# Sample latents turned by VectorE, with the first sequence's chain earlier, and a merge with a filled edge and shorter column sums

## The reference

```
def one_seq(args):
    q_b, pt, c_b, kr_b = args
    c_all = concatenate([cache_latent[layer, pt].reshape(past_len, KV_LORA), c_b])
    kr_all = concatenate([cache_krope[layer, pt].reshape(past_len, QK_ROPE), kr_b])
    k = mla_keys(c_all, kr_all, kpos, w_uk, g_k_mla)      # rms_norm over each head's 96 columns
    return attend_latent(q_b, k, c_all, qpos, kpos, w_uv) # softmax, context in latents, then w_uv
```

```
y = silu(layer_norm(conv(hist) + b_dw, g_ln, b_ln)) @ w_conv_out
x = x + (sig(g_a) * y_mla + sig(g_b) * y_conv + sig(g_c) * y_mem) @ w_out
```

## Time and profile before

| what | value |
|---|---|
| median of 3 runs | 2519.83 us |
| the profiled execution's own time | 2512.91 us |
| its span, first to last instruction | 2511.1 us |
| TensorE busy | 2418.1 us (96%) |
| VectorE, ScalarE, GpSimd busy | 1044.8, 597.2, 768.6 us |
| mean granted TensorE clock | 0.990 |

### The profile page before, as it was taken

One profiled execution on the slowest core, in us unless ns is written; L12 is line 12 of the kernel. 1 busy time (PEld: TensorE's weight loads), 2 busy tenths in 40 slices (PEclk: granted clock), 3 DMA queues, 4 the chain that ended last, 5 costly groups with the idle time before them and its releaser, 6 DMA issues. The chain is left out here.

```text
span 2511.1 us, 35803 instructions
## 1 busy us (share of the span) xinstructions
PE 2418.1 (96%) x12532; PEld 1641.9 (65%) x12532; DVE 1044.8 (42%) x2299; ACT 597.2 (24%) x1193; POOL 768.6 (31%) x574
## 2 busy tenths in 40 slices
PE   7999999999899999999999999989999999999996
PEld 4566666666654555556656666647778777877874
DVE  4233344445524343349964226643333332333331
ACT  2222333334333444210012101201111111112121
POOL 1000000000025555300000005544556555656652
PEclk9999999999999999999999999999999999999998
DMA  8111111011233232063112162048999999999996
GB/s 290 40 41 45 45 45 42 28 31 38 68 113 89 75 90 65 20 192 77 41 51 77 38 208 68 19 178 297 331 332 332 344 352 358 357 363 358 365 353 188
DMA packets 208870, 404.65 MB, mean 161 GB/s; under 512 B 51675, under 2 KB 139024, under 8 KB 192220
## 3 DMA queue, kind: packets, MB, share of 16 engines
q1 hardware_dynamic: 173220, 318.41, 36.1%
q0 software_dynamic: 27936, 72.22, 11.5%
q10 hardware_dynamic: 7536, 11.73, 1.3%
HBM read 342.83 MB, written 70.70 MB: 165 GB/s over the span
## 5 line engine op out<-in xcount | busy, mean ns | idle before, releaser
L2488 POOL DMA_INDIRECT mergedT<-tokens_normed,gather_rows x304 | 309.3, 1018 | 120.5 <-issue 94.8
L2687 PEld LDWEIGHTS pGe<-xT,we_g 128*128 128x128 f32 x2048 | 261.8, 191 | 33.2 <-issue 32.8
L2602 DVE STREAM_TRANSPOSE xT<-mergedT 128x1280 f32<-128x1280 f32 (+2 forms) x64 | 152.7, 2386 | 283.9 <-DMA mergedT<-tokens_normed,gather_rows 263.0
L2687 PE MATMUL pGe<-xT,we_g 128*128 128x128 f32 (+4 forms) x2048 | 270.8, 290 | 0.0
L2687 PE MATMUL pUe<-xT,we_u 128*128 128x128 f32 (+4 forms) x2048 | 267.0, 289 | 0.0
L2687 PEld LDWEIGHTS pUe<-xT,we_u 128*128 128x128 f32 x2048 | 260.7, 191 | 0.0
L1437 PE MATMUL pKs<-ws_uk,cTs 128*128 128x512 f32 x512 | 233.2, 597 | 1.2 <-issue 1.2
L1150 POOL TENSOR_TENSOR rk<-ssk,half 128x32 f32<-128x32 f32 x32 | 173.4, 5428 | 188.5 <-DVE ssk L1279 188.5
L2697 PE MATMUL pYe<-we_d,first_w 128*128 128x512 f32 x512 | 230.2, 592 | 0.8 <-DVE first_w L2608 0.8
L2548 ACT ACTIVATE mergedT<-pYe,wc 128x512 f32<-128x512 f32 x128 | 88.0, 688 | 403.0 <-PE pYe L2697 382.1
L2508 POOL DMA_INDIRECT sums<-mergedT,add_rows x64 | 103.8, 1621 | 229.1 <-issue 91.5
(11 more groups left out here) (452 smaller groups left out, 3272.6 us busy)
## 6 DMA issues: line engine op xcount, KB each, us to landing
we_g<-in_w_e_gate SPq DMA_DIRECT2D x64, 1024.0 KB
we_u<-in_w_e_up SPq DMA_DIRECT2D x64, 1024.0 KB
we_d<-in_w_e_down SPq DMA_DIRECT2D x64, 1024.0 KB
mergedT<-in_cache_latent SPq DMA_DIRECT2D x96, 128.0 KB, 2.1
raw_columns<-fill_out SPq DMA_DIRECT2D x48, 172.0 KB
first_w<-in_w_in SPq DMA_DIRECT2D x12, 512.0 KB, 6.1
branch_w<-in_w_in SPq DMA_DIRECT2D x10, 512.0 KB
mergedT<-tokens_normed,gather_rows POOLq DMA_INDIRECT x304
```

The lines of the kernel that those rows point to most:

```text
L2488: pool.indirect_dma_start(out=xg[v % 2][:, g, :], out_offset=None, in_=quarter, in_offset=bass.IndirectOffsetOnAxis(ap=gi[v % W][:, g:g + ...
L2602: v.transpose(xT[p][:, :, 0:n * GR].rearrange("p c (g i) -> p g c i", g=n), xg[p][:, 0:n, :].rearrange("p g (j c) -> p g c j", c=KD)).then ...
L2687: mm = pe.matmul(dst[p][:, f * CAP:f * CAP + n], w[r][:, k, f * P:(f + 1) * P], xT[p][:, k, 0:n], start=k == 0, stop=k == KD - 1)
```

## The change

In `stage_sample` the latents are loaded twice. Once as before, by GpSimd's queue, for the context product only (two buffers). And once in quarters of 64 columns, each to another 32 partitions of a small ring `lq`, by 4 DMAs per page of 128 rows of 256 bytes: 2 from SyncE and 2 from ScalarE. VectorE's `transpose` turns 32 by 32 blocks of two pages in one instruction and writes `cT`. `w_uk` is loaded with its rows in the matching order. TensorE's `turn` and ScalarE's `take` are gone. The steps of the chain move to other page numbers, the rope part of a sequence is cut in three, and for sequence 0 it begins at n = 2 and the norms at n = 5.

In `stage_merge` the three gates ahead come before unit 24, nearly all remaining taps come in unit 23, VectorE adds channel blocks 0, 1 and 2 of `y` and GpSimd those of the squares, so that `sums` multiplies two blocks in place of four, and the sums come after units 29 and 35.

```diff
 stage_sample
-    W = 3
+    W = 4
+    NB = NPAGE // 2
-        lat.append(c.sb("lat2", [P, NPAGE, LC])[:, :, :])
+        lq = [c.sb(f"lat_quarters{r}", [P, 2, 4, LORA // 4]) for r in range(W)]
+        def quarter_of(page, i):
+            return a["cache_latent"][0][bass.ds(page, 1)].rearrange("o (g s) (i c) -> i (o s) g c", g=4, i=4)[i]
 sync
+                def quarters(t):
+                    b, j = divmod(t, NB)
...
+                    for n in (2 * j, 2 * j + 1):
+                        page = page_of(sp, b, n)
+                        for i in range(2):
+                            sp.dma_start(lq[t % W][i * 32:(i + 1) * 32, n % 2, :, :], quarter_of(page, i)).then_inc(lq_in[t % W], 16)
+                        if t < W or t >= NB:
+                            rope_rows(b, n, page)
...
+                for t in range(NB * DB):
+                    sp.wait_ge(S["cT_ready"], t + 1)
+                    if t + W < NB * DB:
+                        quarters(t + W)
+                    if t % NB == 3:
+                        memory(t // NB)
 gpsimd
+                def latent(b, n):
+                    page = page_of(pool, b, n)
+                    pool.dma_start(lat[b % 2][:, n, 0:LORA], a["cache_latent"][0][bass.ds(page, 1)].rearrange("o s c -> (o s) c")).then_inc(lat_in[b % 2], 16)
                 for b in range(DB):
+                    if b >= 2:
+                        pool.wait_ge(S["ctx_psum"], b - 1)
+                    for n in range(NPAGE):
+                        latent(b, n)
                     for g in range(NG):
                         pool.wait_ge(S["n_ready"], NG * b + g + 1)
 scalar
+                act.wait_ge(S["table_in"], 16)
+                for page_at in range(6):
+                    other_quarters(page_at)     # page_of, then quarters 2 and 3 of the page
                 fill_take(0)
...
-                        if n % 4 == 1 and g + 1 < NG:
-                            take(b, g + 1)
-                        if n == 13 and b + 1 < DB:
-                            take(b + 1, 0)
-                        if n == (2 if b else 9):
+                        if NPAGE * b + n + 9 < NPAGE * DB:
+                            other_quarters(NPAGE * b + n + 9)
+                        if n == (6 if b else 3):
                             rope_squares(b)
-                        if n == 4 and b >= 1:
+                        if n == 5 and b >= 1:
                             memory_exp(b - 1)
-                        if n == 8 and b >= 1:
+                        if n == 10 and b >= 1:
                             exps(b - 1)
 vector
+                def turn(t):
+                    b, j = divmod(t, NB)
+                    v.wait_ge(lq_in[t % W], 128 * (t // W + 1))
...
+                    v.transpose(cT[b % 2][:, :, 2 * j * P:2 * (j + 1) * P].rearrange("p k (x s) -> p x k s", s=32),
+                                lq[t % W][:, :, :, :].rearrange("p n g (k q) -> p (n g) k q", k=KL)).then_inc(S["cT_ready"], 1)
+                        if n % 2 and NB * b + n // 2 + 3 < NB * DB:
+                            turn(NB * b + n // 2 + 3)
# chain of b - 1: scale stays at n = 2; maxima 4 -> 5; maximum 6 -> 7; centre 8 -> 9; context 12 -> 13; finish 14 -> 15
-                        if n == (3 if b else 10):
-                            rope(b)
+                        if n == (4 if b else 2):
+                            own = rope_begin(b)
+                        if n == (6 if b else 3):
+                            rope_rotate(b, own)
+                        if n == (8 if b else 4):
+                            rope_sums(b, own)
+                        for g, at in enumerate((9, 10, 11, 15) if b else (5, 7, 11, 15)):
+                            if n == at:
+                                norms(b, g)
 tensor: turn removed; by_key 4 -> 5, by_head 6 -> 7, share 7 -> 9, contexts 10 -> 12, turn_context 13 -> 15
                 def page(b, n):
-                    pe.wait_ge(S["cT_ready"], NG * b + n // 4 + 1)
+                    pe.wait_ge(S["cT_ready"], NB * b + n // 2 + 1)
 stage_merge
-    U_LAST, U_MEAN, U_VAR = U_C // 2, U_C + 3, U_C + 9
+    U_LAST, U_MEAN, U_VAR = U_C // 2, U_C + 5, U_C + 11
+        partial = [hist[:, i, 0:TOK] for i in range(KC)]
 gpsimd
+                pool.wait_ge(S["tap"], NTAP)
+                pool.wait_ge(S["mean_psum"], 1)
+                for i in range(2):
+                    pool.wait_ge(S["squares"], i + 2)
...
+                    pool.tensor_tensor(partial[2 + i], partial[2] if i else convT[:, 0, :], convT[:, i + 1, :], ALU.add).then_inc(S["partial"], 1)
 vector, behind the last tap of channel block i
+                            if i in (1, 2):
+                                v.wait_ge(S["last_psum"], 1)
...
+                                v.tensor_tensor(partial[i - 1], partial[0] if i == 2 else y[:, 0, :], y[:, i, :], ALU.add).then_inc(S["partial"], 1)
-                    step = (3 if u < KC - 1 else 5 - (u % 5 == 0)) if u < U_C else 4
+                    step = 1 if u >= U_C else NTAP - 3 - done if u == U_C - 1 else 3 if u < KC - 1 else 5 - (u % 5 == 0)
-                    if u == U_C - 1:
+                    if u == U_C + 3:
                         v.wait_ge(S["last_psum"], 1)      # and the two copies of the last rows
 tensor
+                pe.wait_ge(first_b_in, 16)                # the three gates ahead, now before unit 24
+                for g, (at, n) in enumerate(GROUPS):
+                    pe.wait_ge(S["sig_ready"], U_C - 3 + g + 1)
+                    for k in range(KD):
+                        pe.matmul(pG[g][:, 0:n], keep.first_w[:, k, :], keep.hT[:, k, at:at + n], start=k == 0, stop=k == KD - 1)
-                        sums(y, 0).then_inc(S["mean_psum"], 1)          # was at b == KD
+                        sums(partial[1], y, 0).then_inc(S["mean_psum"], 1)    # at b == KD + 1
-                        sums(convT, DB).then_inc(S["var_psum"], 1)      # was at b == KD + 2
+                        sums(partial[3], convT, DB).then_inc(S["var_psum"], 1) # at b == KD + 3
```

More of the change, by code:

```diff
@@ L1065, in fill_bank @@
             return pK[u % 2 if u < EARLY or u == NFILL - 1 else (u + 1) % 2]
-        lat_in = [[c.sem(f"s_lat_in{p}_{g}") for g in range(NG)] for p in range(W)]
+        lat_in = [c.sem(f"s_lat_in{p}") for p in range(2)]
+        lq_in = [c.sem(f"s_lq_in{r}") for r in range(W)]
         kr_in = [c.sem(f"s_kr_in{p}") for p in range(2)]
@@ L1108, in _ @@
-                for n in range(NPAGE):
-                    rope(0, n, page_of(0, n))
-                memory(0)
-                sp.wait_ge(S["fill_psum"], 3)
-                late_weights(2)
-                for b in range(1, DB):
-                    if b >= W:
-                        sp.wait_ge(S["ctx_psum"], b - W + 1)
-                    if b >= 2:
-                        sp.wait_ge(S["rot_ready"], b - 1)
-                        sp.wait_ge(S["kr_sq"], b - 1)
-                        sp.wait_ge(S["mkT_psum"], b - 1)
-                    for n in range(NPAGE):
-                        page = page_of(b, n)
-                        latent(b, n, page)
-                        rope(b, n, page)
-                    memory(b)
+                quarters(0)
@@ L1266, in rope, with rope_sums @@
                     v.tensor_tensor(krot[:, :, 16:32], kc[:, :, 16:32], ks[:, :, 0:16], ALU.add).then_inc(S["rot_ready"], 1)
+                def rope_sums(b, own):
                     v.wait_ge(S["kr_sq"], b + 1)
@@ L1339, in finish @@
                     v.tensor_tensor(ctxT[:, :, :, b], pX[:, 352:368].rearrange("p (k h) -> p k h", k=KL), spread(rden[:, :], KL), ALU.mult).then_inc(S["ctxT_ready"], 1)
+                for t in range(3):
+                    turn(t)
                 for b in range(DB):
@@ L1532, in _ @@
                 fill(3)
-                turn(0, 0)
                 for b in range(DB):
@@ L1841, in out, with sums @@
                     mm.then_inc(S["unit_psum"], 1)
-                def sums(src, col):
+                def sums(partial, src, col):
+                    blocks = (partial, src[:, KC - 1, :])
                     for at in (0, 512):
-                        for i in range(KC):
-                            pe.matmul(pM[:, at:at + 512], ones[:, :], src[:, i, at:at + 512], start=i == 0, stop=i == KC - 1)
-                    for i in range(KC):
-                        mm = pe.matmul(pMs[:, col:col + DB], ones[:, :], src[:, i, SEQ:TOK], start=i == 0, stop=i == KC - 1)
+                        for i in range(2):
+                            pe.matmul(pM[:, at:at + 512], ones[:, :], blocks[i][:, at:at + 512], start=i == 0, stop=i == 1)
+                    for i in range(2):
+                        mm = pe.matmul(pMs[:, col:col + DB], ones[:, :], blocks[i][:, SEQ:TOK], start=i == 0, stop=i == 1)
                     return mm
```

146 lines of the change are left out of this document (76 added, 70 removed).

## The result

The changed kernel takes 2501.55 us (median of 4 runs, 2495.67 to 2502.96), the kernel before in the same runs 2518.95: ratio 0.9933, 95% interval 0.9919 to 0.9948. That is 17.4 us faster, half of the 35 us forecast.

A forecast was written before the change was run, and what follows sets the result against it. TensorE was taken to bound the page loop. 27.8 (transposes) + 1.2 + 3.7 - 2 - 7 + 11.4 = 35.1 us off the 2519.8 us median gave 2485 us; own range 2474 to 2496, 8-in-10 range 2475 to 2512.

The forecast's parts named there:

- A: Page loop: GpSimd's list bounds at the gathers' pitch, 1.30 us a load; 26 us lost, 2511 us; chance 0.09.
- C: Page loop: ScalarE's issues hold SyncE's, issuing queues set the pace, 41.2 us a sequence; 19 us lost, 2504 us; chance 0.10.
- 2 us of friction: Whole page loop: cost taken for ScalarE's issues and friction of this kind, bounds 0 and 16 us.
- lags by a turn at most: Page loop ahead of n = 5: SyncE's issues, 35.8 of 38.45 us a sequence, fall behind one turn at most; cost 0.
- At most 25 of 38. Hidden: Page loop: DMA engines' work per sequence, 12.6 us plus 6 to 12 for new packets, costs nothing.
- The ring of 4 turns covers it: Page loop ahead of n = 5: four turns of quarter rows absorb SyncE's lag; cost 0.
- about 1 us to spare: Page loop: rope rows issued behind the turn at n = 1, needed at n = 4, arrive with that margin.
- the step that decides: Page loop, GpSimd: 16 loads of 1.0 us (lower bound 0.76) join 21.7 us of powers, 37.7 under 38.45; cost 0.
- B: Page loop: GpSimd serial, register load waits for the running DMA, 1.54 us a load; 53 us lost, 2538 us; chance 0.07.
- Rival D: Sample stage: some other wait, at n = 4 for rope rows or at start, eats 25 us or more; 2515 us; chance 0.04.
- Start, -7 + 1.2 us: Start of sample stage: 5 us wait and 2 us low clock lost; 1.2 us wait for the first copy gained.
- Merge, 11.4 us: Merge stage: 7.7 us gained from halved sums, 3.7 at the edge; GpSimd's two additions taken as 0.

The follow-up runs named there:

- e5: Changed kernel with a ring of six turns of quarter rows in place of four: 0.9860, 2482.02 us.
- e13: Changed kernel without GpSimd's page loads for sequences 2 to 7: 0.9874, 2487.82 us.
- e15: Changed kernel, ring of four, memory loads behind turn 6 and GpSimd's page loads spread, eight of them paced by TensorE's pages: 0.9860, 2484.48 us.
- e12: Changed kernel, ring of four, rope rows of sequences 2 to 7 not loaded, so SyncE issues two DMAs per page, not three: 0.9932, 2499.30 us.
- e1: New sample stage with the merge of the kernel before: 0.9965, 2507.29 us.
- e4: Changed kernel with the chain's steps behind the first maxima one to two pages later: 0.9897, 2491.58 us.
- e2: Sample stage of the kernel before with the new merge: 0.9978, 2511.27 us.
- e6: Changed kernel with a ring of six, chain steps one page later, two weight loads moved to turns 12 and 20, ScalarE's first issues spread: 0.9862.
- e9: Changed kernel, ring of six but ScalarE nine pages ahead, its first issues spread, two merge iterations with five taps for four: 0.9881, 2485.36 us.
- e11: Changed kernel, ring of six, ScalarE's first issues spread, two weight loads moved to turns 12 and 20: 0.9858, 2480.74 us.
- e16: Changed kernel, SyncE ring of six, ScalarE nine pages ahead, start spread, weight loads moved, GpSimd's loads spread as in e15: 0.9850, 2481.58 us.
- e17: e15 with sequence 1's rope steps two pages later, ScalarE's first issues spread, two weight loads moved: 0.9855, 2482.40 us.
- e10: e5 with each GpSimd page load split into two halves, 32 loads per sequence in place of 16: 1.0103, 2541.25 us.

## Why the prediction was wrong, point by point

The time lies inside the range of 2475 to 2512 us, but above the forecast's own 2474 to 2496. Above 2496 the range was there for rivals A and C, and neither's cause was found: that it holds the time is luck.

**Transposes off TensorE, 27.8 us: right, and 2 us better.** Where nothing is late a sequence takes 38.20 us (`e5`, `e13`, `e15`) against 41.93, and sequence 0 31.0 against 34.4: about 29.9 us in all.

**The failed step** is the loop's cost of waits, put at 2 us of friction. Where nothing is late the first, a middle and the last sequence take 31.0, 38.2 and 32.3 us in the changed kernel and 34.4, 41.9 and 36.6 in the one before. Beyond these, waits and low clock take 26.3 us of the loop in after and 3.9 in before. The loop from first to last page went from 327.7 to 320.2 us, 7.5 gained where 27.8 + 3.7 - 2 = 29.5 were forecast. Of the 26.3 us, 17.3 are in sequences 2 to 7 and gone in `e13`, so the burst makes them. The other 9.0 are in sequence 1 and stay in `e13` (8.8): there the sentence that SyncE "lags by a turn at most" failed first, by 4.5 us of late issue. Two sentences carried the rest. "At most 25 of 38. Hidden" was right as an average (the measured share is 0.55 of 41.3 us, 22.7 us) and wrong as an argument: the work of a resource has a time as well as a size, and 12 us of each sequence are at a share of 1.00. "The ring of 4 turns covers it" counted issue times and not landings: 1.7 us outside the burst, 5.8 inside. The burst itself comes from the step of GpSimd's loads and from the memory's, which SyncE issues at the same place. I asked only whether GpSimd's loads fit into its list, and they fit the better the denser they go out.

**Rope rows, "about 1 us to spare", and "the two pK banks give that about 2 us":** half right. VectorE waited for the rows in six sequences, 15.2 us in all, 7.9 of them in sequence 1. But VectorE's lateness did not reach TensorE through the banks (0.2 us). It came through the chain's two maxima, which stand behind those waits in VectorE's list. I had not named what is queued behind VectorE's wait.

**SyncE, ScalarE, VectorE, right in size:** 2.12 us a page, issues of 0.32 to 0.35 us with 10 of 584 over 1 us, and a transpose at 0.70 us in place of 1.12.

**GpSimd, "the step that decides": it didn't.** A load takes 0.54 us where prepared ahead and 1.14 where not, 0.65 on average in after. That is under the lower bound of 0.76: the bound took every load's register part to be in series, and part of them is prepared while powers run. A and B fall.

**Rival C had the right number (41.2 us a sequence) for a wrong reason:** issues did not grow, and with a third of SyncE's taken away (`e12`) the periods stayed at 38.7 to 43.5 us. The Trainium skill ("Perfetto Trace Analysis", section DMA Instruction — HWDGE (DVE, Sync)) has an issue lock the shared generator and counts the wait for it in the recorded duration, so such waits would have shown as long issues. The trace has them only now and then, the longest 1.6 us. Rival D, another wait at n = 4, was nearest in mechanism and had 0.04; its 2515 us were too many.

**Packets of 256 bytes: inside the bounds.** They take 18.7 ns each in the loop (60672 of them), those of 4096 bytes 222 ns, so 13.7 against 18.4 bytes per ns. The Trainium skill ("DMA: Bandwidth & Descriptors", section Specifications) says that transfers under 512 bytes miss line rate. The trace agrees in direction, and packets of 256 bytes lose a quarter of the rate here.

**Start, -7 + 1.2 us: measured -3.1.** The first page came at 711.46 in place of 708.37. Ahead of the loop the clock stood at the lower level for 17.1 us in one stretch in place of 10.2 (mean 0.74 against 0.86 up to the loop). `e1`, `e4` and `e5` have the same start and 10.2 us, and reach the loop 35.7 to 35.9 us after the stage's first product, against 35.5 in before and 38.6 in after. But `e2`, with the start of before, took 38.4 us. So the issues ahead of `fill_take(0)` cost little by themselves, and how much of the 3 us is theirs and how much the clock's own variation isn't shown. Spread, they gave 33.2 to 36.3 us (`e6`, `e9`, `e11`, `e16`, `e17`).

**Merge, 11.4 us: measured 8.5.** The sums gave 7.76 as forecast. The waits of the edge were 2.20 and 0.40 us (forecast 1.8 and 1.1) and 0.58 at unit 15 (forecast 1.0). GpSimd's additions, costed at 0, cost 1.81 us of TensorE's time through VectorE; their own 3.2 and 2.5 us were inside the bounds, and the harm was beside them. 5.2 + 2.4 - 2.2 - 0.4 - 0.6 = 4.4 at the edge, with 7.8 for the sums and -1.8, would be 10.4; 1.9 us in many short waits I can't place.

**The mixer**, up to the first product of the routed experts, gave 2.0 us back (242.3 to 244.3 us), with 13.7 us at the low clock in place of 3.4. The same stretch took 241.6 us in `e1`, with the merge of before, and 241.2 to 244.8 us in the other runs, with the clock low for 3.4 to 13.7 us. Whether the change makes the long stretches likelier isn't shown.

In sum: 22.0 us missing in the loop, 2.9 in the merge, 2.0 in the mixer, 2.7 better at the start, 24.2 of the 24.6 between 35.1 and the 10.5 us that the two profiled executions differ by. The medians differ by 17.4; the profiled execution of before lies below all its timed runs.

## What to carry to other kernels

A share of DMA time per period says that it fits, not that it is on time: lay the transfers of one period side by side and look for the stretch at a share near 1, above all where one queue can issue many large transfers in a row that nobody needs for a long time. Where an in-order engine waits for data that is needed late, the price is what stands behind the wait in its list; a deeper ring (`e5`) or bulk loads paced by the consumer's progress (`e15`) took that price away here. And a rival that predicts the right total isn't shown by the total.

## What the hardware showed that I had not expected

- GpSimd prepares DMAs while its engine is busy: the register loads of 12 DMAs ran beside four powers (`e10`), and 21 issues then went out 0.535 us apart, against 1.14 us when the register load and address stood between.
- An issue's landing went from 1.7 to 6.8 to 7.4 us while 289 to 294 GB/s moved; small transfers are held up by bulk ones that another queue issued. Without GpSimd's loads they landed after 1.9 to 2.4 us at the same place (`e13`).
- While GpSimd added two operands in SBUF, VectorE's instructions with both operands in SBUF took 1.97 us in place of 0.52 and 3.40 in place of 1.23, and ended 0.4 and 1.1 us behind GpSimd's; one with an operand in PSUM took 0.51 beside it. This is as the Trainium skill has it ("SBUF — State Buffer", section SBUF: two separate sides): the port that the two engines share is held for a whole instruction, and a VectorE instruction wants it when both its inputs are in SBUF.
